# adaLN gates spread over the tokens through DRAM instead of TensorE transposes, in a two-layer streaming encoder

## What is computed

```python
mod = jax.nn.silu(c) @ w_ada + b_ada
sh1, sc1, ga1, sh2, sc2, ga2, sh3, sc3, ga3 = [m[:, None, :] for m in jnp.split(mod, 9, axis=-1)]
h = rms_norm(x, gains[0]) * (1 + sc1) + sh1
x = x + MACARON_W * ga1 * rms_norm(swiglu(h, w_f1_in, w_f1_out), gains[1])
h = rms_norm(x, gains[2]) * (1 + sc2) + sh2
y, rows = token_mixing(h, ..., w_in, w_gate, b_gate, g_gla, w_out)
x = x + ga2 * rms_norm(y, gains[3])
h = rms_norm(x, gains[4]) * (1 + sc3) + sh3
x = x + MACARON_W * ga3 * rms_norm(swiglu(h, w_f2_in, w_f2_out), gains[5])
```

## Time and profile before

| | us |
|---|---|
| median of 3 runs | 1605.83 (1605.77 to 1606.11) |
| span of the profiled execution | 1603.4 |
| PE busy | 1576.6 (98%) |
| DVE busy | 800.3 (50%) |
| ACT busy | 586.6 (37%) |
| POOL busy | 151.3 (9%) |
| DMA, HBM read | 258.70 MB, 165 GB/s over the span |

### The profile page before, as it was taken

How to read it: one execution, slowest core, us unless ns; L and a number is a source line. 1 busy time by engine, 2 the same in 40 slices (tenths; PEclk the granted TensorE clock), 3 DMA queues, 4 the chain that set the end, 5 groups by cost and what they waited for, 6 DMA issues and landing times.

```text
span 1603.4 us, 26160 instructions
## 1 busy us (share of the span) xinstructions
PE 1576.6 (98%) x10238; PEld 1436.5 (90%) x10238; DVE 800.3 (50%) x1210; ACT 586.6 (37%) x814; POOL 151.3 (9%) x225
## 2 busy tenths in 40 slices
PE   5999999999999999999999999999999999999998
PEld 4999998889997899998889999987999879999987
DVE  3434442468657734443374344326675675444424
ACT  4322222264455522222272222224635554222223
POOL 5000000010242000000010000000105300000000
PEclk9999999999999999999999999999999999999999
DMA  9877744653346576444557744355533363444332
GB/s 345 252 229 214 235 132 157 211 171 106 106 137 212 172 235 196 131 131 150 183 180 224 240 128 131 131 184 184 150 109 123 101 220 105 131 131 131 130 118 81
DMA packets 254151, 266.03 MB, mean 166 GB/s; under 512 B 11727, under 2 KB 216653, under 8 KB 254066
## 3 DMA queue, kind: packets, MB, share of 16 engines
q1 hardware_dynamic: 231968, 183.52, 38.2%
q0 software_dynamic: 22080, 81.26, 14.7%
q10 hardware_dynamic: 18, 0.04, 0.0%
HBM read 258.70 MB, written 6.09 MB: 165 GB/s over the span
## 4 chain that ended last, share of the span: by engine, by line
PE 92%; DVE 3%; ACT 2%; DMA 1%; DVEq 1%; SPq 1%; issue 0%; ACTq 0%
PE ps L1984 15%; PE ps L1985 15%; PE ps L1989 15%; PE ps L2045 8%; PE ps L2047 8%; PE ps L2049 8%; PE ps L1956 4%; PE ps L1957 4%; PE ps L1958 4%; PE ps L1898 2%; DMA w_ada_g<-in_w_ada_dram 1%; PE ps L1975 1%; DVE x L1392 1%; PE ps L1971 1%; PE ps L2062 1%; PE ps L1972 1%
## 5 line engine op out<-in xcount | busy, mean ns | idle before, releaser
L1298 DVE TENSOR_TENSOR w_lo<-w_raw,w_hi 128x2048 fp32r<-128x2048 f32 x158 | 363.8, 2302 | 238.5 <-ACT w_hi L905 207.8
L1984 PE MATMUL ps<-act_hi,w_hi 128*128 128x384 f32 x1344 | 452.1, 336 | 0.0
L1985 PE MATMUL ps<-act_lo,w_hi 128*128 128x384 f32 x1344 | 449.4, 334 | 0.0
L905 ACT ACTIVATE w_hi<-w_raw 128x2048 fp32r<-128x2048 f32 x128 | 245.3, 1916 | 229.0 <-PE ps L2049 226.9
L1984 PEld LDWEIGHTS ps<-act_hi,w_hi 128*128 128x128 f32 x1344 | 252.2, 188 | 6.6 <-issue 6.6
L1985 PEld LDWEIGHTS ps<-act_lo,w_hi 128*128 128x128 f32 x1344 | 252.4, 188 | 0.0
L1989 PE MATMUL ps<-act_hi,w_lo 128*128 128x384 f32 x1344 | 246.5, 334 | 0.0
L984 ACT ACTIVATE silu_g<-ps 128x384 f32<-128x384 f32 x88 | 43.4, 493 | 537.1 <-PE ps L1989 536.2
L1989 PEld LDWEIGHTS ps<-act_hi,w_lo 128*128 128x128 f32 x1344 | 234.2, 188 | 0.0
L1459 DVE TENSOR_TENSOR hid_f<-silu_g,ps 128x384 f32<-128x384 f32 x88 | 48.8, 554 | 366.6 <-ACT silu_g L984 366.6
L2045 PE MATMUL ps<-w_hi,hid_hi 128*128 128x512 f32 x480 | 148.7, 391 | 0.0
(11 more groups left out here) (422 smaller groups left out, 1717.8 us busy)
## 6 DMA issues: line engine op xcount, KB each, us to landing
w_raw<-in_w_ffn_in_dram SPq DMA_DIRECT2D x176, 512.0 KB, 5.1
w_ada_sb<-in_w_ada_dram POOLq DMA_DIRECT2D x45, 1024.0 KB, 7.1
w_raw<-in_w_ffn_out_dram SPq DMA_DIRECT2D x88, 512.0 KB, 4.2
w_raw<-in_w_in_dram SPq DMA_DIRECT2D x46, 512.0 KB, 4.6
w_ada_g<-in_w_ada_dram POOLq DMA_DIRECT2D x16, 1024.0 KB, 5.5
w_raw<-in_w_out_dram SPq DMA_DIRECT2D x16, 512.0 KB, 5.4
w_ada_g<-in_w_ada_dram SPq DMA_DIRECT2D x5, 1024.0 KB, 15.3
w_ada_s<-in_w_ada_dram POOLq DMA_DIRECT2D x3, 1024.0 KB, 9.8
```

Source lines behind the costliest of these rows:

```text
L905: act.activation(w_hi[slot][:], w_raw[slot][:], ACT.Copy).then_inc(hi_ready.sem, 1)
L1298: dve.tensor_tensor(w_lo[slot][:], w_raw[slot][:], w_hi[slot][:].bitcast(F32), ALU.subtract).then_inc(lo_ready.sem, 1)
L1984: pe.matmul(ps[:, bank + half, 0:N], w, act_hi[:, f, :], start=(f == 0), stop=False)
L1985: pe.matmul(ps[:, bank + half, 0:N], w, act_lo[:, f, :], start=False, stop=False)
```

## The change

`mod`'s 72 columns of a gate component (8 chunks by 9 sequences) are turned as they stand, by one transpose for a component: `turn_gates` writes [72, 128] to the free half of PSUM bank 7. In `proj_out` of norm 0 that is done for the gates of norms 0 and 1 (two transposes), in `proj_out` of norm 2 for its own gate (one); both stand behind the first unit, where `gates_to_tokens(nth, 0)` stood. DVE copies the rows to `gate_rows`, which is `ada_rows`' space (`copy_gate_rows`). POOL stores them to a DRAM tensor `gates` (`store_gates`: 36 KB a component), waits for the landing, and loads `gate_tok` by two DMAs of 512 KB with a repeating source (`load_gate`: the samples' rows 16 times each, the prompt's row 128 times). In norm 1 only `load_gate(1)` is left. DVE's `renorm` waits for the landing. `gates_to_tokens`, `spread_gate`, `read_gate` and ACT's two copies are gone.

```diff
+                def store_gates(norms):
+                    pool.wait_ge(gate_rows_ready.sem, gate_rows_ready.at(l, norms[0] // 2 + 1))
+                    pass_gate()
+                    for c, nth in enumerate(norms):
+                        pool.dma_start(gates[l, nth].rearrange("s (f n) -> f s n", n=P),
+                                       gate_rows[:, c, :]).then_inc(gate_rows_stored.sem, 16)
+                    pool.wait_ge(gate_rows_stored.sem, gate_rows_stored.at(l, norms[-1] + 1))
+                    pass_gate()
+                def load_gate(nth):
+                    pool.dma_start(gate_tok[:, 1, :], gates[l, nth, 1:NSEQ, :].unsqueeze(1).broadcast_to([B, S, D])).then_inc(gate_landed.sem, 16)
+                    pool.dma_start(gate_tok[:, 0, :], gates[l, nth, 0:1, :].broadcast_to([P, D])).then_inc(gate_landed.sem, 16)
...
                     for k, units in ((3, 3), (4, 6), (5, 8), (6, 8)):
+                        if k == 5:
+                            store_gates(norms)
+                            load_gate(norms[0])
                         pool.wait_ge(unit_used.sem, unit_used.at(l, u0 + units))
                         ada_load(m + k, layer, components[k // 4])
...
+                pool.wait_ge(unit_used.sem, unit_used.at(l, U_WOUT + 1))
+                pass_gate()
+                load_gate(1)
                 pool.wait_ge(unit_used.sem, unit_used.at(l, U_WOUT + 2))
...
                 def renorm(nth):
 
                     left, right = slice(0, 512), slice(512, 1024)
+                    dve.wait_ge(gate_landed.sem, gate_landed.at(l, 2 * nth + 2))
...
-                    spread_gate(nth)
-                    read_gate(nth, 0)
+                    copy_gate_rows(nth // 2, 2 - nth // 2)
                     split_lo(u0 + units - 2, (u0 + units - 2) % 2)
-                    read_gate(nth, 1)
                     split_lo(u0 + units - 1, (u0 + units - 1) % 2)
...
+                def turn_gates(n, components):
+                    pe.wait_ge(gain_folded, (FOLD_F1, FOLD_GAP2)[n][l])
+                    for c, component in enumerate(components):
+                        m = pe.transpose(ps[0:KD * NSEQ, ADA_BANK_B, 256 + c * P:256 + (c + 1) * P],
+                                         mod[:, component, :, :].rearrange("p f s -> p (f s)"), ident[:])
+                    m.then_inc(gate_turned.sem, 1)
...
-                    gates_to_tokens(nth, 0)
+                    turn_gates(nth // 2, ((2, 5), None, (8,))[nth])
                     for u in range(1, units - 2):
...
-                    gates_to_tokens(nth, 1)
                     last_two(u0 + units - 2, (2 * units - 4, 2 * units - 2), hid_hi, hid_lo, nth, lambda n: None)
```

More of the change, by code:

```diff
@@ L323, in encoder_program @@
         ps = ctx.enter_context(nc.psum_tensor("ps", [P, 8, 512], F32))
+        gates = nc.dram_tensor("gate_rows_dram", (DEPTH, 3, NSEQ, D), F32, kind="Internal").ap()
+        gate_rows = ada_rows[0:KD * NSEQ, :].rearrange("r (c n) -> r c n", n=P)
         def sig(name, per_layer, step=1, start=0, before=0):
@@ L382, in encoder_program @@
         FOLD_HEAD, FOLD_F1, FOLD_GAP1, FOLD_GAP2, FOLD_F2, FOLD_GAP3 = 1, (2, 7), (3, 8), (4, 9), 5, 6
-        gate_tr = sig("gate_tr", 6)
-        gate_read = sig("gate_read", 6)
-        gate_spread = sig("gate_spread", 3)
+        gate_turned = sig("gate_turned", 2)
+        gate_rows_ready = sig("gate_rows_ready", 2)
+        gate_rows_stored = sig("gate_rows_stored", 3, 16)
+        gate_landed = sig("gate_landed", 6, 16)
         head_copied = sig("head_copied", 1)
@@ L721, in ada_loop, with ada_gap @@
                                            .rearrange("(k p) n -> p k n", p=P)).then_inc(ada_landed[slot], 16)
-                def ada_gap(n, layer, components, u0):
+                def store_gates(norms):
[9 more added lines that the diff above has]
+                    pool.dma_start(gate_tok[:, 0, :], gates[l, nth, 0:1, :].broadcast_to([P, D])).then_inc(gate_landed.sem, 16)
+                def ada_gap(n, layer, components, u0, norms):
                     m = 4 * n
@@ L735, in _ @@
                 ada_loop(n0, l, component, count)
[L736 removed]
+                ada_gap(N_GAP1[l], l, GAP_F1[l], U_F1OUT, (0, 1))
                 pool.wait_ge(ada_used, 4 * N_GAP2[l])
@@ L840, in _ @@
                     ada_loop(N_F2, l + 1, LOOP_F2[0], len(LOOP_F2))
-                    ada_gap(N_GAP3, l + 1, GAP_F2, U_F2OUT)
+                    ada_gap(N_GAP3, l + 1, GAP_F2, U_F2OUT, (2,))
+                else:
+                    store_gates((2,))
+                    load_gate(2)
             pool.wait_ge(rows_stored.sem, rows_stored.at(DEPTH, 0))
@@ L1195, in _ @@
                 act.wait_ge(gla_lo.sem, gla_lo.at(l, HB))
-                for n in range(2):
-                    act.wait_ge(gate_tr.sem, gate_tr.at(l, 2 + n + 1))
-                    if n == 0:
-                        act.wait_ge(gate_spread.sem, gate_spread.at(l, 2))
-                    act.activation(gate_tok[:, n, :], ps[:, 6:8, :].rearrange("p a n -> p (a n)"), ACT.Copy).then_inc(gate_read.sem, 1)
-                    if n == 0:
-                        split_first_hi(U_F2IN, U_WOUT + 1)
+                split_first_hi(U_F2IN, U_WOUT + 1)
                 renorm(1)
@@ L1441, in renorm, with copy_gate_rows @@
                     normalise(2, x_normed, right)
-                def spread_gate(nth):
-                    dve.drain()
-                    dve.tensor_copy(spare_tok[:].rearrange("p (f b t) -> p f b t", f=KD, t=S), per_seq(3 * nth + 2)).then_inc(gate_spread.sem, 1)
-                def read_gate(nth, n):
-                    dve.wait_ge(gate_tr.sem, gate_tr.at(l, 2 * nth + n + 1))
-                    dve.tensor_copy(gate_tok[:, n, :], ps[:, 6:8, :].rearrange("p a n -> p (a n)")).then_inc(gate_read.sem, 1)
-                    dve.drain()
+                def copy_gate_rows(n, comps):
+                    dve.wait_ge(gate_turned.sem, gate_turned.at(l, n + 1))
+                    dve.tensor_copy(gate_rows[:, 0:comps, :], ps[0:KD * NSEQ, ADA_BANK_B, 256:256 + comps * P]
+                                    .rearrange("r (c n) -> r c n", n=P)).then_inc(gate_rows_ready.sem, 1)
                 def hidden(u0, h0, j, s):
@@ L2050, in tile_products, with last_two @@
                     return m
-                def gates_to_tokens(nth, n):
-                    if n == 0:
-                        folded = ((FOLD_F1[0], FOLD_GAP3)[l], FOLD_F1[l], FOLD_GAP2[l])[nth]
-                        pe.wait_ge(gain_folded, folded)
-                    else:
-                        pe.wait_ge(gate_read.sem, gate_read.at(l, 2 * nth + 1))
-                        pe.wait_ge(gate_spread.sem, gate_spread.at(l, nth + 1))
-                    for f in range(KD):
-                        rows = mod[:, 3 * nth + 2, f, 0:1].broadcast_to([P, P]) if n == 0 else spare_tok[:, f * P:(f + 1) * P]
-                        m = pe.transpose(ps[:, 6 + f // 4, (f % 4) * P:(f % 4 + 1) * P], rows, ident[:])
-                    m.then_inc(gate_tr.sem, 1)
-                def last_two(u, chunks, src_hi, src_lo, nth, ready, turn_gates=None):
+                def turn_gates(n, components):
[4 more added lines that the diff above has]
+                    m.then_inc(gate_turned.sem, 1)
+                def last_two(u, chunks, src_hi, src_lo, nth, ready):
                     def products(n, k):
@@ L2089, in last_two @@
                     products(0, 1)
-                    if turn_gates is not None:
-                        turn_gates()
                     ready(1)
@@ L2100, in last_two @@
                     last_products(2, (0,))
-                    pe.wait_ge(gate_read.sem, gate_read.at(l, 2 * nth + 2))
+                    if nth != 1:
+                        pe.wait_ge(gate_rows_ready.sem, gate_rows_ready.at(l, nth // 2 + 1))
                     banks = SAMPLE_BANKS_F2 if nth == 1 else SAMPLE_BANKS
```

6 lines of the change are left out of this document (1 added, 5 removed).

## The result

| | before | changed |
|---|---|---|
| median, us | 1605.97 (1605.77 to 1607.05) | 1635.76 (1629.67 to 1637.67) |
| span of the profiled execution | 1603.4 | 1632.7 |
| ratio of the times, 95% interval | | 1.018 (1.0168 to 1.0192) |

A forecast was written before the change was run, and what follows sets the result against it. PE, busy 98% of the span, was taken as the bound. 1603.4 - 10.2 (PE net) + 3.8 (tails given back) = 1597.0 us of span, plus 2.4 for the runs' median: 1599.4 us; range 1595.8 to 1606.5.

The forecast's parts named there:

- PE's loss of blocks, 10.2 us net: On PE, 12 blocks of eight transposes go (10.9 us) and six single transposes come (0.7 us).
- DVE's and ACT's copies are worth nothing; the new copy takes 0.35.: Copies removed from DVE and ACT stand ahead of waits, so save nothing; DVE's new 0.35 us copy is covered too.
- The store's landing, 2.5 us: On POOL, the second gate store lands 2.5 us after issue, between 1.8 quiet and 4.9 loaded; load_gate issues at 302.0.
- m+5 to m+7 some 0.5 to 1.5 us later.: POOL's loads behind its wait for the stores go 0.5 to 1.5 us later; PE uses them at 334.31, nobody waits.
- c, the delay of the first unit: 1.5 us: In norm-0 tails the added load delays the next stage's first unit 1.5 us (0.85 in norm 2); 3.8 us lost together.
- half the engines: Rival: the samples' load, with 8 distinct rows, runs on 8 of 16 engines, 1.25 us more at three places; 1603.2, chance 0.18.
- repeated reads are slow: Rival: 128 reads of one 4 KB row run at half pace, 7.7 us over three places; 1607.1, chance 0.10.
- the pause takes it, nobody waits: In the mixing block, load_gate(1) goes 8.2 us before its use into the DMA pause before the next stage's weights; nothing lost.
- `renorm`'s new wait costs nothing.: On DVE, the gate lands by some 306 and is first wanted at about 319: 13 us of room.
- the narrow and the slow cases: Rivals: half the engines, 1603.2 (0.18); repeated reads at half pace, 1607.1 (0.10), or a third, 1614.7 (0.07).
- The signs of being wrong.: Wrong if renorm's first step waits for the gate's DMA, POOL's stores take over 5 us, or first_hi is no later.
- all of it stays: Rival: SP's load gets its turn beside POOL's, c about 0, only 0.4 us lost; 1596.0, chance 0.20.

The follow-up runs named there:

- The fastest version: Changed kernel with DVE's copy behind its first two split_lo, POOL's stores and loads behind m+3, and the samples' rows widened in DRAM first; 1595.11 us.
- The first early version: Changed kernel with stores and loads of norms 0 and 2 behind POOL's wait for three units, DVE's copy ahead of its split_lo loop; 1627.85 us.
- The two kernels without loads: Changed kernel with load_gate's DMAs replaced by memsets: stores first, 1601.45 us; m+5 and m+6 issued first, 1596.69 us.
- the widened versions: Changed kernel with the samples' rows written 16 times in DRAM, then loaded from 128 different rows; early 1595.11 us, late 1595.75 us.
- The late one: Changed kernel with the widening in DRAM alone, everything staying at the change's place between m+4 and m+5; 1595.75 us.
- the one with eight small DMAs: The first early version with the samples' load cut into eight DMAs of 16 partitions, one for each sample; 1616.03 us.

## Why the prediction was wrong, step by step

- **PE's loss of blocks, 10.2 us net.** Right. The fastest version's span is lower by 10.3, and the account of the changed kernel closes with 10.2 to within 1 us. The estimate of 24.8 us from the 275 ns of the Trainium skill (TensorE: Matmul & The Clock Gate, Part 4: PE-mode transpose) is not borne out as a cost: the rows show the same duration, but eight in a row take 0.79 us.
- **DVE's and ACT's copies are worth nothing; the new copy takes 0.35.** Right (0.41 us, no one waits). The first early version shows that this hangs on the copy's place in DVE's order.
- **The store's landing, 2.5 us.** Too small: POOL's wait behind the second issue was 3.7 us. I chose a value near the quiet end of the earlier trace rows because the store is small; its engines were under load, and the loaded end of 4.9 was as near. The load went at 304.65 in place of 302.0: 1.2 us of that is the landing, 0.7 the time from the copy's end to POOL's first issue, and 0.6 the second store's issue, which I had not counted.
- **"m+5 to m+7 some 0.5 to 1.5 us later."** The step that failed first. They were 2.9 us later (305.83 against 302.97), and I looked only at who uses them, PE at 334. That SP's unit waits behind them I had said, but I priced only the load that is added ahead of it, not the later start of these 2 MB. The two kernels without loads put a price of 4.8 us on this alone (1601.45 against 1596.69).
- **c, the delay of the first unit: 1.5 us.** The term that was mis-sized. Measured, less the later start of that stage (0.2 at SP's issue): 322.10 - 314.97 - 0.2 = 6.9 in the first tail. The pause that the load was to fill was empty because the load came only at 304.65, and behind it 2 MB stood closer to SP's issue. With plain loads c is 320.88 - 314.97 - 1.0 = 4.9, and without loads it is 318.12 - 314.97 - 0.3 = 2.8. So of the 6.9 us, 2.8 come from POOL's hold, 2.1 from 1 MB of plain load and 2.0 from the narrow pattern. The mistake was there before the narrow load came in, and with plain loads the forecast of 1599.4 would have missed too (1610.22 measured).
- **The rival "half the engines", 1603.2, and its chance of 0.18.** The right pattern, and the wrong size. I priced only the load's own longer run, 1.25 us at three places. In the runs the sum of all traffic falls to about half while it is under way, the two mixing blocks wait as well, and it costs 24 us. It should also have been the forecast, since the Trainium skill's rule (DMA: Bandwidth & Descriptors, Rules for kernel authors) speaks of an outermost dimension below 16, which this load has, and no row spoke against it. "Nothing in the trace tests it" was taken as a reason for a low chance; it was only a reason for a wide range.
- **Rival "repeated reads are slow".** Not the cause, by two single executions: with 128 repeats of one row in place of different rows the time is 1635.76 against 1635.34 (the prompt's load) and 1612.26 against 1610.22 (the samples'), where this rival had 7.7 us. A lower rate in the windows beside it is there, as shown above.
- **The mixing blocks: "the pause takes it, nobody waits".** Half right. With plain rows PE waits in neither. With the narrow load they wait 8.1 and 5.4 us, the former the longest of the five, as the first unit of `w_ffn_in` follows and two units' time does not cover it. I took 1 MB as 2.55 us there without a second price.
- **`renorm`'s new wait costs nothing.** Right in the form it had: L1397 follows `first_lo` at once. The way in which the change could lose, a late first unit, was thus named rightly. The range ended at 1606.5 because the narrow and the slow cases were priced apart and never together with the held loads.
- **The signs of being wrong.** None of the three came: `renorm` did not wait for the gate, the stores landed in under 5 us, and `first_hi` was later. They could not tell a loss of 1 us from one of 7. What did not fit was PE's wait: forecast at 1 to 2 us before the prompt's transposes in three tails, found at 5.35 to 8.09 us before the samples' in five.
- **The clock.** Missing from the prediction altogether: 8.5 us behind 30.8 us of waits, more than a quarter on top.
- **Rival "all of it stays", 1596.0.** It is what the widened versions give, 1595.11 and 1595.75. They take the whole of 10 us, so the idea of the change is sound, and its pattern and order of DMAs are not. The late one owes it partly to luck: its longer hold happened to push the 2 MB behind SP's issue, which its own expectation had as a cost.

## What to carry to other kernels

When a DMA is added, list every DMA that is issued within some microseconds behind it, on any queue, and ask which of those has a waiter; who uses the added data is the smaller question. Look at the outermost dimension of both patterns of a DMA: here 128 was quick and 8 was slow, and eight small DMAs with 16 were between. Where a broadcast makes it small, widening the data in DRAM first cost nothing that could be told here. A wait for a landing in front of unrelated loads reorders these loads against the other queues, which can cost more than the wait, or nothing, by where they then fall: move the wait, then look at the neighbours.

## What the hardware showed that I had not expected

- With 512 KB loads of an outer dimension of 8, the median from issue to landing is 8.1 us (over twelve, six of them narrow), where it is 4.6 with 128 in all, and while such a load runs the sum of all DMAs falls to 205 to 254 GB/s from 377 and more, with the DMA share still near 1.
- One row of 4 KB read for 128 partitions costs the kernel at most 2 us over 128 different rows (single executions), though a window beside it shows 213 GB/s in place of 336.
- PE's granted clock is 0.50 behind a wait of 5.55 us, and the next 1.6 us of transposes and the products behind them run at half pace. In the first early version it falls behind one of four waits of 2.6 to 2.7 us, and in the one with eight small DMAs behind two of four.
- A 36 KB store lands after a median of 3.9 us at the changed kernel's place, 2.0 where it is issued ahead of m+3 (the first early version), 4.8 right behind m+3 (the widened one), and 6.5 right behind m+5 and m+6.
- Eight DMAs of 64 KB, each with 16 rows of one source row, were no full replacement of a plain load. That stays open.
